# Passes of 512 weight columns in the second block's values and output projections

## The chip, the cores and the metric

The kernel runs on one core of one Trainium2 chip. The metric is the device time of one execution in microseconds (us); the median of several runs is compared.

## The reference

One sequence of 256 tokens of width 1024 goes through two blocks in float32. The first block (adaptive norm, a mixer of three kinds of attention, a convolutional feed-forward part) isn't touched by the change. The second block is two layers, each with a residual and a layer norm:

```python
def second_block(x, gla_w_in, ..., ln_g, ln_b):
    for layer in range(DEPTH_2):                       # DEPTH_2 = 2
        if layer < N_A_LAYERS:                         # N_A_LAYERS = 1
            y = gla_mixer(x, ...)
        else:
            if layer == N_A_LAYERS:
                k_sh, v_sh = shared_kv(x, w_kv)
            y = dilated_mixer(x, swa_w_in[i], swa_w_out[i], k_sh, v_sh)
        x = layer_norm(DEEPNORM_ALPHA * x + y, ln_g[layer], ln_b[layer])

def gla_mixer(x, w_in, w_a2, b_a2, norm_g, w_out):
    proj = x @ w_in                                    # q 512, k 512, v 1024, g 1024, a_lr 16
    log_a = jax.nn.log_sigmoid(a_lr @ w_a2 + b_a2) / 16
    o = gla_chunked(q, k, v, log_a)                    # 4 heads, chunks of 64 tokens, a decaying state
    o = o * lax.rsqrt(jnp.mean(o * o, axis=-1, keepdims=True) + RMS_EPS)
    return (o * norm_g * jax.nn.silu(g)) @ w_out

def shared_kv(x, w_kv):
    k, v = jnp.split(x @ w_kv, [768], axis=-1)         # 3 groups x 2 heads x 128, each
    return rope(k, pos), v

def dilated_mixer(x, w_in, w_out, k_sh, v_sh):
    q, g = jnp.split(x @ w_in, [3072], axis=-1)        # 3 groups x 8 heads x 128, and the gate
    ...                                                # windowed attention with dilation 1, 4, 16
    return (o * jax.nn.silu(g)) @ w_out
```

## The kernel before

All weights are read from HBM in chunks of about 1 MB (128 partitions x 2048 elements), in an order fixed in `STREAM`, into a ring of four buffers `raw`. To compute in fp32r with the accuracy of float32, each chunk is split in two: ScalarE (ACT) copies it rounded to `whi` (`high`, L639), VectorE (DVE) computes the remainder `wlo = raw - whi` (`low`, L1052). The activations are split the same way (`hhi`/`hlo`, `gohi`/`golo`, `ohi`/`olo`). TensorE (PE) then adds three products per tile (`three`, L1596 to L1598): high by high, low by high, high by low. There are three pairs of split buffers (chunk c uses `whi[c % 3]`, but chunk GOUT+3 uses `wgo` and the last chunk `hhi`/`hlo`) and three result banks `res0` to `res2` in PSUM, taken in turn. `bank(r)` (L1600) lets PE wait until result r-3 has been drained by ACT or DVE. `FIRST_RESULT`, `RESULT_MARK`, `RESULT_DRAIN` and `CHUNK_MARK` (L119 to L134) are the counts of the semaphores `product_done`, `drained_act` and `drained_dve` on which everybody waits.

A chunk is 1024 rows by 256 columns. It makes 48 passes on PE: in `fm` the weights are stationary and the 256 tokens move (the result has features on partitions); in `tm` a tile of 128 tokens is stationary and the 256 weight columns move, once for each of two token tiles, so that the result has tokens on partitions. The chunks of the second block, in order: GK (2), GA, GQ (2), GV (4, values), GG (4, gates), GOUT (4, output projection), SK (3, shared keys), SV (3, shared values), SWA (16, queries and gates), SOUT (4, output projection). GV, GOUT, SV and SOUT have tokens as their stationary tile.

Every engine has its own program, a loop over the chunks in the order above; what stands in it ahead of an instruction is always done first. ACT's step for chunk c is the weight copy of chunk c+3, then what drains result c. In the GV stage PE also makes four transposes (L1974) after GV+2 and the small products of the attention within 16-token blocks (L1982) after GV+3, for which DVE has to finish the factors `gfacs`; ACT computes their exponentials (L900, L903) between the copies, and the copy `kdT` (L906). In the GOUT stage PE first adds the residual by products with the identity (`residual`, L1722) to each bank. The token tiles are normalised one after the other (`rows_normed`, `row_sum`, `row_squares`), transposed back by PE (`hidden`, L1730) and split again (L710, L1479) before SK can begin; 23 products that nobody reads (`warm`, L1644) lie between the end of tile 1 and its transposes.

```python
            def bank(r):
                if r >= DIRECT + NB:
                    who, n = RESULT_DRAIN[r - NB]
                    pe.wait_ge(drained[who], n)
                return res[r % NB]
```

## Time and profile before

| what | value |
|---|---|
| median of 3 runs | 753.12 us (752.69 to 759.79) |
| profiled execution, first to last instruction | 757.1 us |
| PE busy | 730.8 us (97%) |
| weight loads busy | 710.5 us (94%) |
| DVE busy | 524.7 us (69%) |
| ACT busy | 396.1 us (52%) |
| GpSimd busy | 104.3 us (14%) |
| read from HBM | 139.17 MB, 185 GB/s over the span |

The profiled execution is one of its own; of it the span is known, and it is 4 us above the median of the runs. Durations below are from it. A matmul's duration in the trace is its latency, and the next one starts before it ends, so what a pass costs is read from the distance of two starts. A plain f32 product appears as two records.

### The profile page before, as it was taken

How to read it: one execution, taken by the hardware profiler on the slowest of the kernel's cores; microseconds unless marked ns; L12 is line 12 of the kernel's file. 1: busy time of each engine (PE TensorE's matmuls, PEld its weight loads, DVE VectorE, ACT ScalarE, POOL GpSimd, SP SyncE). 2: the span in 40 equal slices, each digit the busy share in tenths (PEclk: the TensorE clock that was granted, in tenths of full speed). 3: DMA queues.
4: the chain of work that ended last, by engine and by line, in shares of the span. 5: the costliest groups of instructions: out<-in, count | busy, mean ns of one | idle time of the engine just before them, and what ended most of it. 6: DMA issues, size and time to landing. Idle time of an engine off the chain costs nothing.

```text
span 757.1 us, 14222 instructions
## 1 busy us (share of the span) xinstructions
PE 730.8 (97%) x5964; PEld 710.5 (94%) x5964; DVE 524.7 (69%) x778; ACT 396.1 (52%) x560; POOL 104.3 (14%) x87
## 2 busy tenths in 40 slices
PE   8899999998899999999999999999999999999995
PEld 6799899898898999999999989899999999999995
DVE  4979888886977678777767556925576347555665
ACT  4286455545364544544544348528555456556551
POOL 0130000000522000000001130000004455443000
PEclk9999999999999999999999999979999999999998
DMA  8995567555363455654566544514446553343101
GB/s 343 411 356 190 203 268 274 193 204 219 113 244 146 167 200 190 213 178 161 204 261 233 205 138 148 207 66 168 167 154 223 184 206 117 116 159 112 57 1 56
DMA packets 22265, 141.13 MB, mean 186 GB/s; under 512 B 2389, under 2 KB 3029, under 8 KB 6458
## 3 DMA queue, kind: packets, MB, share of 16 engines
q1 hardware_dynamic: 21626, 137.28, 50.1%
q0 software_dynamic: 576, 2.95, 1.0%
q8 instruction: 47, 0.77, 0.4%
q14 instruction: 16, 0.13, 0.1%
HBM read 139.17 MB, written 1.05 MB: 185 GB/s over the span
## 4 chain that ended last, share of the span: by engine, by line
PE 70%; DVE 13%; issue 7%; ACT 5%; DMA 3%; POOL 0%; SPq 0%; DVEq 0%; ACTq 0%
PE res L1596 20%; PE res L1598 19%; PE res L1597 19%; ACT whi L639 3%; DVE wlo L1052 3%; PE pX L1803 2%; DMA shared<-in_w_ada 1%; PE pS L1783 1%; PE pX L1982 1%; DVE shared L1065 1%; DVE raw L1065 1%; DMA y<-in_w_ada 1%; ACT sq L654 1%; PE pT L1793 1%; PE pS L1644 1%
## 5 line engine op out<-in xcount | busy, mean ns | idle before, releaser
L1596 PE MATMUL res<-hhi,whi 128*128 128x256 f32 (+1 forms) x1120 | 318.9, 285 | 4.1 <-DVE wlo L1052 1.5
L1052 DVE TENSOR_TENSOR wlo<-raw,whi 128x2048 fp32r<-128x2048 f32 (+3 forms) x101 | 229.1, 2270 | 126.4 <-ACT whi L639 126.2
L1597 PE MATMUL res<-hhi,wlo 128*128 128x256 f32 (+1 forms) x1120 | 312.9, 279 | 0.0
L1598 PE MATMUL res<-hlo,whi 128*128 128x256 f32 (+1 forms) x1120 | 312.8, 279 | 0.0
L639 ACT ACTIVATE whi<-raw 128x2048 fp32r<-128x2048 f32 (+3 forms) x101 | 188.3, 1865 | 120.2 <-issue 87.1
L1596 PEld LDWEIGHTS res<-hhi,whi 128*128 128x128 f32 (+1 forms) x1120 | 209.6, 187 | 5.9 <-issue 3.4
L1597 PEld LDWEIGHTS res<-hhi,wlo 128*128 128x128 f32 (+1 forms) x1120 | 209.4, 187 | 0.4
L1598 PEld LDWEIGHTS res<-hlo,whi 128*128 128x128 f32 (+1 forms) x1120 | 209.4, 187 | 0.2
L538 POOL TENSOR_TENSOR sq<-sq,rope 128x512 f32<-128x512 f32 x18 | 39.5, 2195 | 78.5 <-ACT sq L654 78.5
L1596 PE MATMUL res<-uhi,whi 128*128 128x256 f32 x176 | 49.3, 280 | 0.0
L1597 PE MATMUL res<-uhi,wlo 128*128 128x256 f32 x176 | 49.1, 279 | 0.0
L1598 PE MATMUL res<-ulo,whi 128*128 128x256 f32 x176 | 49.1, 279 | 0.0
L1065 DVE CUSTOM_DVE_ANT_0 raw<-raw,cact,cols 128x1024 f32<-128x1024 f32 x32 | 41.8, 1344 | 0.0
L1596 PE MATMUL res<-whi,hhi 128*128 128x256 f32 x144 | 40.5, 281 | 0.0
L1597 PE MATMUL res<-whi,hlo 128*128 128x256 f32 x144 | 40.1, 278 | 0.0
L1598 PE MATMUL res<-wlo,hhi 128*128 128x256 f32 x144 | 40.1, 278 | 0.0
L1598 PEld LDWEIGHTS res<-ulo,whi 128*128 128x128 f32 x176 | 33.1, 188 | 0.0
L1596 PEld LDWEIGHTS res<-uhi,whi 128*128 128x128 f32 x176 | 33.0, 188 | 0.0
L1597 PEld LDWEIGHTS res<-uhi,wlo 128*128 128x128 f32 x176 | 32.9, 187 | 0.0
L560 POOL TENSOR_TENSOR sq<-sq 128x512 f32<-128x512 f32 x4 | 7.6, 1902 | 182.6 <-ACT sq L863 167.0
L802 ACT ACTIVATE up<-shared,unmax 128x128 f32<-128x128 f32 (+1 forms) x24 | 10.9, 456 | 41.4 <-DVE unmax L1207 41.4
L576 POOL TENSOR_TENSOR y<-y,sq 128x512 f32<-128x512 f32 x8 | 10.5, 1351 | 140.4 <-DVE sq L1227 140.4
(334 smaller groups left out, 1211.1 us busy)
## 6 DMA issues: line engine op xcount, KB each, us to landing
raw<-in_wts SPq DMA_DIRECT2D x97, 1024.0 KB, 5.0
raw<-in_w_ada SPq DMA_DIRECT2D x16, 1024.0 KB, 5.1
shared<-in_w_ada SPq DMA_DIRECT2D x6, 1024.0 KB, 11.1
gates<-in_wts SPq DMA_DIRECT2D x4, 768.0 KB, 13.3
raw<-in_wts SPq DMA_DIRECT2D x4, 768.0 KB, 5.6
y<-in_w_ada SPq DMA_DIRECT2D x2, 1024.0 KB, 9.2
x<-in_xT SPq DMA_DIRECT2D x2, 512.0 KB, 4.7
gv<-in_ln_rows POOLq DMA_DIRECT2D x1, 1024.0 KB, 7.5
```

The lines of the kernel that those rows point to most:

```text
L538: nc.gpsimd.tensor_tensor(xsw, xsw, table[:, 1:2, :].to_broadcast([P, 2, T]), ALU.mult).then_inc(sin_done, 1)
L560: nc.gpsimd.tensor_tensor(sq[:, 0:2, :], sq[:, 0:2, :], sq[:, a:a + 2, :], ALU.add).then_inc(presummed, 1)
L576: nc.gpsimd.tensor_tensor(y[:, 2 * j:2 * j + 2, :], y[:, 2 * j:2 * j + 2, :], gtmp[:, n % 4, :].rearrange("p (a b) -> p a b", a=2), ALU.ad ...
L639: nc.scalar.activation(hi[:, 0:kt * w], raw[RAW_OF["w", c] % RAW][:, 0:kt * w], ACT.Copy).then_inc(hi_ready, 1)
L654: nc.scalar.activation(swapped(c)[a:a + block_rows, :, :].rearrange("p a b -> p (a b)"), ps[b:b + block_rows, :], ACT.Copy).then_inc(moved ...
L802: nc.scalar.activation(up[:, s % 3, 0:nk], usc[:, s % 2, 0:nk], ACT.Exp, scale=-1.0, bias=unmax[:, s % 4:s % 4 + 1], accum_out=uden[:, s % ...
L1052: nc.vector.tensor_tensor(lo[:, 0:b], raw[RAW_OF["w", c] % RAW][:, 0:b], hi[:, 0:b].bitcast(f32), ALU.subtract).then_inc(lo_ready, 1)
L1065: nc.vector.tensor_tensor_reduce(out=w[:, D * i:D * i + D], in0=w[:, D * i:D * i + D], in1=cact[:, :], op0=ALU.mult, op1=ALU.add, scale=1. ...
L1596: mm(out, ah, bh, start=first, stop=False)
L1597: mm(out, al, bh, start=False, stop=False)
L1598: return mm(out, ah, bl, start=False, stop=last)
L1803: last = mm(pX[:, T + P * t:T + P * t + P], v, dpT[:, t, P * i:P * i + P], start=i == 0, stop=i == 3)
```

## The change

In GV, GOUT, SOUT and the first two chunks of SV a chunk is now 512 rows (four k-tiles) by 512 columns, in place of 1024 rows by 256. A pass moves 512 columns, so a pair of chunks needs 48 passes where it needed 96, and fills one whole bank for each token tile. A result is complete after the second chunk of a pair: the first chunk of a GV or SV pair marks no result (`results_of` is 0), the second marks two. ACT moves both results of a pair after it. GOUT keeps tile 0's and tile 1's first halves open together for six k-tiles, then finishes tile 0's first half, its second half, tile 1's first half, its second half. SOUT goes k-tile by k-tile over both token tiles for the first 512 columns, then tile by tile. The sums of the layer norm are made over 512 columns at once in place of twice 256. Removed lines are left out of the diff where the old functions above show them.

```diff
@@ -84,7 +84,14 @@
         return 2, 1024
     if DOWN <= c < GK:
         return (8, 8, 6)[(c - DOWN) % 3], 256
+    if in_rows(c):
+        return 4, 512
     return KT, 256
+
+
+def in_rows(c):
+
+    return GV <= c < GG or GOUT <= c < SK or SV <= c < SV + 2 or SOUT <= c
 
 
 def results_of(c):
@@ -93,7 +100,9 @@
         return 4
     if DOWN <= c < GK:
         return 2 if (c - DOWN) % 3 == 2 else 0
-    return 2 if c == SK - 1 else 1
+    if GV <= c < GG or SV <= c < SV + 2:
+        return 2 * ((c - (GV if c < GG else SV)) % 2)
+    return 1
 
 
...
@@ -130,7 +139,7 @@
     CHUNK_MARK.append(_m)
 
 
-CHUNK_MARK[GOUT + 1] = RESULT_MARK[FIRST_RESULT[GOUT + 3]]
+CHUNK_MARK[GOUT] = CHUNK_MARK[GOUT + 1] = CHUNK_MARK[GOUT + 2]
 CHUNK_MARK[GOUT + 2] = CHUNK_MARK[GOUT + 3]
 
...
@@ -196,16 +205,18 @@
         return cols(gla_in, 3072, 16)
     if c < GV:
         return cols(gla_in, 256 * (c - GQ), 256)
+    if in_rows(c):
+        m, first, a = ((gla_in, GV, 1024) if c < GG else (gla_out, GOUT, 0) if c < SK else
+                       (w_kv, SV, 768) if c < SWA else (swa_out, SOUT, 0))
...
@@ -883,11 +894,11 @@
                     own(nc.scalar.activation(gla, glz, ACT.Abs))
                     own(nc.scalar.activation(gla, gla, ACT.Exp, scale=-1.0))
                     nc.scalar.activation(gla, gla, ACT.Ln, bias=1.0).then_inc(loga_ready, 1)
-                if GV <= b < GG:
-                    j = b - GV
-                    ps = result(FIRST_RESULT[b])
-                    nc.scalar.activation(gv[:, :, 256 * j:256 * j + 256], ps[:, :].rearrange("p (t n) -> p t n", t=2),
-                                         ACT.Copy).then_inc(drained_act, 1)
+                if b in (GV + 1, GV + 3):
+                    j = (b - GV) // 2
+                    for t in range(2):
+                        ps = result(FIRST_RESULT[b] + t)
+                        nc.scalar.activation(gv[:, t, 512 * j:512 * j + 512], ps[:, :], ACT.Copy).then_inc(drained_act, 1)
                 if b == GV - 1:
 
...
@@ -943,32 +954,24 @@
                         act.wait_ge(go_full, i + 1)
                         nc.scalar.activation(gohi[:, 2 * i:2 * i + 2, :], y[:, 2 * i:2 * i + 2, :], ACT.Copy).then_inc(go_hi, 1)
                 if b == GOUT:
+                    load_root()
+                if b in (GOUT, GOUT + 2):
+                    t = (b - GOUT) // 2
+                    row_sum(result(FIRST_RESULT[b])[:, :], t, 0, 512, 0).then_inc(drained_act, 1)
+                    act.wait_ge(z_shift, t + 1)
+                    row_squares(z[:, t, 0:512], t, 0, 3).then_inc(z_squared, 1)
+                    if t:
+                        high(SK)
+                        hidden_high(0)
+                if b in (GOUT + 1, GOUT + 3):
+                    t = (b - GOUT) // 2
                     ps = result(FIRST_RESULT[b])
+                    row_sum(ps[:, :], t, 512, 512, 2).then_inc(z_summed, 1)
+                    row_squares(ps[:, :], t, 512, 4).then_inc(drained_act, 1)
+                    row_root(t, 0)
+                    if t:
+                        hidden_high(1)
+                        high(SK + 1)
                 if b == SOUT + 1:
                     load_root()
...
@@ -1481,18 +1485,18 @@
 
                 if b == GOUT:
                     low(c + 2)
+                if b in (GOUT, GOUT + 2):
+                    t = (b - GOUT) // 2
+                    dve.wait_ge(drained_act, RESULT_DRAIN[FIRST_RESULT[b]][1])
+                    shift_of(t)
+                    if t:
+                        low(SK)
+                        hidden_low(0)
                 if b == GOUT + 1:
                     dve.wait_ge(rows5_in, 16)
                     dve.wait_ge(xe_ready, 1)
                     rows_normed(0, 0, gv, x_rows, x_rows_ready)
                 if b == GOUT + 3:
                     rows_normed(1, 0, gv, x_rows, x_rows_ready)
                     hidden_low(1)
...
@@ -1505,14 +1509,12 @@
                     low(c + 2)
                     dve.wait_ge(x_ready, 2)
                 if SOUT <= b < SOUT + 2:
+                    t = b - SOUT
+                    row_add(result(FIRST_RESULT[b])[:, :], t, 0, 512, 0).then_inc(drained_dve, 1)
                     dve.wait_ge(drained_dve, RESULT_DRAIN[FIRST_RESULT[b]][1])
+                    shift_of(t)
+                    if t:
+                        dve.wait_ge(rows_in, 16)
                 if b >= SOUT + 2:
                     t = b - SOUT - 2
...
@@ -1711,10 +1713,22 @@
                     last = mm(out, meanw[:, :], sq[:, k, :], start=False, stop=k == 7)
                 last.then_inc(mean_known[n], 1)
 
-            def token_product(ps, at, t, k, ih, il, wh, wl, first, last):
-
-                return three(ps[:, at:at + T], ih[:, k, t * P:t * P + P], il[:, k, t * P:t * P + P],
-                             wh[:, k, :], wl[:, k, :], first, last)
+            def rows_product(ps, t, first_c, k, ih, il, first, last):
+
+                wh, wl = weights_of(first_c + k // 4)
+                return three(ps[:, :], ih[:, k, t * P:t * P + P], il[:, k, t * P:t * P + P],
+                             wh[:, k % 4, :], wl[:, k % 4, :], first, last)
+
+            def rows_chunk(c, first_c):
+
+                wait_weights(c)
+                r, kg = FIRST_RESULT[first_c + 1], c - first_c
+                for t in range(2):
+                    ps = res[(r + t) % NB] if kg else bank(r + t)
+                    for k in range(4 * kg, 4 * kg + 4):
+                        last = rows_product(ps, t, first_c, k, hhi, hlo, k == 0, k == KT - 1)
+                    if t or kg:
+                        last.then_inc(product_done, 1)
 
             def residual(ps, at, t, ks):
...
@@ -2004,43 +2018,38 @@
                     r = FIRST_RESULT[GOUT]
                     if c == GOUT:
                         pe.wait_ge(xe_ready, 1)
+                        first = bank(r), bank(r + 2)
                         for t in range(2):
+                            residual(first[t], 0, t, range(4))
+                            for k in range(6):
+                                if k % 4 == 0:
+                                    wait_weights(GOUT + k // 4)
+                                pe.wait_ge(go_lo, k // 2 + 1)
+                                rows_product(first[t], t, GOUT, k, gohi, golo, False, False)
+                        pe.wait_ge(go_lo, 4)
+                    if c in (GOUT, GOUT + 2):
+                        t = (c - GOUT) // 2
+                        for k in (6, 7):
+                            last = rows_product(first[t], t, GOUT, k, gohi, golo, False, k == 7)
+                        last.then_inc(product_done, 1)
+                    if c in (GOUT + 1, GOUT + 3):
+                        t = (c - GOUT) // 2
+                        ps = bank(FIRST_RESULT[c])
+                        residual(ps, 0, t, range(4, KT))
                         for k in range(KT):
+                            if k % 4 == 0:
+                                wait_weights(GOUT + 2 + k // 4)
+                            last = rows_product(ps, t, GOUT + 2, k, gohi, golo, False, k == 7)
+                            if t and k == 5:
+                                hidden(0)
                         last.then_inc(product_done, 1)
+                        if t:
+                            warm(23, ident, pX[:, 0:P])
+                            hidden(1)
                 elif c < SOUT:
+                    if SV <= c < SV + 2:
+                        rows_chunk(c, SV)
+                    elif c == SV + 2:
                         tm(c, hhi, hlo)
                     else:
...
@@ -2050,22 +2059,22 @@
                 else:
                     r = FIRST_RESULT[SOUT]
                     if c == SOUT:
+                        first = [bank(r + t) for t in range(2)]
                         for k in range(KT):
+                            if k % 4 == 0:
+                                wait_weights(SOUT + k // 4)
                             pe.wait_ge(d_lo, k // 2 + 1)
+                            for t in range(2):
+                                last = rows_product(first[t], t, SOUT, k, ohi, olo, k == 0, k == 7)
+                                if k == 7:
                                     last.then_inc(product_done, 1)
                     if c == SOUT + 2:
                         for t in range(2):
                             ps = bank(r + 2 + t)
+                            for k in range(KT):
+                                if k % 4 == 0:
+                                    wait_weights(SOUT + 2 + k // 4)
+                                last = rows_product(ps, t, SOUT + 2, k, ohi, olo, k == 0, k == 7)
                             last.then_inc(product_done, 1)
```

ACT's row in the GV stage, before; `whi2<-raw0` is the weight copy for GV+3, `whi0<-raw1` that for GG, `gfacs` with 3072 elements the exponential, `gv<-res1` the move of GV's result:

```order
L639 ACTIVATE whi2<-raw0 128x2048 [waits lo_ready,product_done,raw_full0]
L889 ACTIVATE gv<-res1 128x2x256 [waits product_done]
L903 ACTIVATE gfacs<-gfacs 128x3072 [waits gdiff]
L639 ACTIVATE whi0<-raw1 128x2048 [waits lo_ready,product_done,raw_full1]
L889 ACTIVATE gv<-res2 128x2x256 [waits product_done]
L639 ACTIVATE whi1<-raw2 128x2048 [waits lo_ready,product_done,raw_full2]
L889 ACTIVATE gv<-res0 128x2x256 [waits product_done]
L906 ACTIVATE kdT<-pT 128x512 [waits kd_T]
```

And now:

```order
L650 ACTIVATE whi2<-raw0 128x2048 [waits lo_ready,product_done,raw_full0]
L914 ACTIVATE gfacs<-gfacs 128x3072 [waits gdiff]
L650 ACTIVATE whi0<-raw1 128x2048 [waits lo_ready,product_done,raw_full1]
L901 ACTIVATE gv<-res1 128x512 [waits product_done]
L901 ACTIVATE gv<-res2 128x512 [waits product_done]
L650 ACTIVATE whi1<-raw2 128x2048 [waits lo_ready,product_done,raw_full2]
L917 ACTIVATE kdT<-pT 128x512 [waits kd_T]
```

The move of GV's result no longer stands ahead of the exponential; both results of the first pair are moved behind it and behind the weight copy for GG.

PE from chunk GV+2 on, now; `res0` and `res1` are the banks of its two token tiles, L1988 are the four transposes, and `...` stands for passes of the same kind:

```order
L1598 MATMUL res0<-whi1,hhi 128x512 [waits drained_act,lo_ready]
L1599 MATMUL res0<-whi1,hlo 128x512
L1600 MATMUL res0<-wlo1,hhi 128x512
...
L1600 MATMUL res0<-wlo1,hhi 128x512
L1598 MATMUL res1<-whi1,hhi 128x512 [waits drained_act]
L1599 MATMUL res1<-whi1,hlo 128x512
L1600 MATMUL res1<-wlo1,hhi 128x512
...
L1988 MATMUL pT<-ident,gfacs 128x128 [waits gfac]
L1988 MATMUL pT<-ident,gfacs 128x128 x3
L1598 MATMUL res0<-whi2,hhi 128x512 [waits lo_ready]
```

The second token tile waits for `drained_act`, that is, for the move out of `res1` just shown; before, GV+2 took one bank for both tiles and waited once.

PE at the start of GOUT, before; the first row is the last pass of GG+3:

```order
L1598 MATMUL res2<-hlo,whi0 128x256
L1722 MATMUL res0<-ident,xe 128x128 [waits drained_act,xe_ready]
L1722 MATMUL res0<-ident,xe 128x128 x3
L1596 MATMUL res0<-whi1,gohi 128x256 [waits go_lo,lo_ready]
L1597 MATMUL res0<-whi1,golo 128x256
L1598 MATMUL res0<-wlo1,gohi 128x256
```

And now:

```order
L1600 MATMUL res2<-hlo,whi0 128x256
L1736 MATMUL res0<-ident,xe 128x128 [waits drained_act,xe_ready]
L1736 MATMUL res0<-ident,xe 128x128 x3
L1598 MATMUL res0<-whi1,gohi 128x512 [waits go_lo,lo_ready]
L1599 MATMUL res0<-whi1,golo 128x512
L1600 MATMUL res0<-wlo1,gohi 128x512
```

The wait for `drained_act` at the first residual is now for two banks, that of tile 0 (`res0`) and that of tile 1 (`res2`, which holds the result of GG+3); before it was for `res0` alone.

## Rows read from the trace of the kernel before

**Rows 1.** The page: busy time of each engine, and the granted clock in 40 slices.
```profile
PE 730.8 (97%) x5964; PEld 710.5 (94%) x5964; DVE 524.7 (69%) x778; ACT 396.1 (52%) x560; POOL 104.3 (14%) x87
...
PEclk9999999999999999999999999979999999999998
```

**Rows 2.** Busy times of stretches: busy us (x instructions) of PE, PEld, DVE, ACT, POOL, PEclk, DMA, GB/s.
```profile
240.00:340.00 100.00, 100.00 (x851) 100.00 (x850) 76.79 (x92) 51.96 (x50) 3.80 (x5) 1.00 0.52 180
...
464.00:486.00 22.00, 20.94 (x183) 20.74 (x182) 21.97 (x22) 17.11 (x15) 0.00 (x0) 1.00 0.54 175
...
590.00:625.00 35.00, 35.00 (x297) 34.91 (x296) 16.27 (x12) 17.51 (x18) 15.13 (x9) 1.00 0.54 187
```

**Rows 3.** Plain f32 products of 256 columns: timeline row, and durations min/median/max in ns.
```profile
514.78 1.89 PE L1811 MATMUL pT<-tb,headw 128*128 128x256 f32 x8
...
L1811 PE MATMUL pT<-tb,headw x8: 378/379/379, 514.8 to 516.3; 128*128 128x256 f32 x8
```

**Rows 4.** Timeline of ACT (start us, us, engine, line, operation, idle before and releaser), 472 to 481.
```profile
472.92 0.57 ACT L889 ACTIVATE gv<-res 128x512 f32<-128x512 f32 x1
...
475.46 2.78 ACT L903 ACTIVATE gfacs<-gfacs 128x3072 f32<-128x3072 f32 x1 [1.97 <-DVE gfacs L1376]
...
478.14 1.91 ACT L639 ACTIVATE whi<-raw 128x2048 fp32r<-128x2048 f32 x1
...
479.95 0.58 ACT L889 ACTIVATE gv<-res 128x512 f32<-128x512 f32 x1
```

**Rows 5.** Timeline of PE at the end of GV+2 and the start of L1982.
```profile
478.00 0.28 PE L1596 MATMUL res<-whi,hhi 128*128 128x256 f32 x1
...
478.34 0.28 PE L1596 MATMUL res<-whi,hhi 128*128 128x256 f32 x1
...
478.69 0.60 PE L1974 MATMUL pT<-ident,gfacs 128*128 128x128 f32 x4
...
486.37 10.32 PE L1982 MATMUL pX<-qI,gfacs 128*16 128x16 f32 x125 [1.43 <-DVE gfacs L1400]
```

**Rows 6.** Busy times of stretches around the two falls of the granted clock.
```profile
498.30:500.10 1.80, 1.80 (x10) 1.76 (x9) 1.77 (x10) 0.00 (x0) 0.00 (x0) 0.51 0.00 0
...
749.60:752.60 3.00, 0.00 (x0) 0.00 (x0) 2.70 (x9) 1.11 (x3) 0.00 (x0) 1.00 0.34 127
...
752.80:757.00 4.20, 0.00 (x0) 0.00 (x0) 1.73 (x4) 0.00 (x0) 0.00 (x0) 0.50 0.34 125
```

**Rows 7.** PE's waits: waited for, us in total, times, longest us.
```profile
PE res L1596 <- ACT gates L779: 1.9, 1, 1.9
```

**Rows 8.** Timelines of PE and ACT at the start of the gated layer's output projection.
```profile
530.64 1.05 PE L1722 MATMUL res<-ident,xe 128*128 128x128 f32 x8
...
532.53 0.63 ACT L944 ACTIVATE gohi<-y 128x512 fp32r<-128x512 f32 x1 [2.48 <-DVE y L1438]
...
533.55 0.83 ACT L921 ACTIVATE gs<-res,ggh 128x256 f32<-128x256 f32 x2
```

**Rows 9.** Timelines of PE, ACT and DVE at the end of both token tiles.
```profile
546.91 0.61 PE L1722 MATMUL res<-ident,xe 128*128 128x128 f32 x4
...
557.76 0.60 ACT L696 ACTIVATE tb<-res 128x512 f32<-128x512 f32 x1 [1.42 <-PE res L1598]
...
557.61 1.28 DVE L1479 TENSOR_TENSOR hlo<-pS,hhi 128x512 fp32r<-128x512 f32 x2
...
558.81 0.20 DVE L1452 TENSOR_SCALAR zs<-zs 128x1 f32<-128x1 f32 x1
```

**Rows 10.** Timelines of PE and DVE in the last projection.
```profile
726.17 0.28 PE L1596 MATMUL res<-whi,ohi 128*128 128x256 f32 x1
...
749.02 0.28 PE L1598 MATMUL res<-hlo,ohi 128*128 128x256 f32 x1
...
743.72 0.69 DVE L1501 CUSTOM_DVE_ANT_0 tb<-res,x 128x512 f32<-128x512 f32 x1 [3.98 <-PE res L1598]
...
749.34 0.69 DVE L1501 CUSTOM_DVE_ANT_0 tb<-res,x 128x512 f32<-128x512 f32 x1 [0.33 <-PE res L1598]
```

More of the change, by code:

```diff
@@ L1457, in rows_normed @@
                     if base == 0:
-                        dve.wait_ge(drained_act, RESULT_DRAIN[FIRST_RESULT[SK - 1] + t * 2 - 1][1])
+                        dve.wait_ge(drained_act, RESULT_DRAIN[FIRST_RESULT[GOUT + 1 + 2 * t]][1])
                     else:
@@ L2006, in _ @@
                         pe.wait_ge(xe_ready, 1)
-                        ps = bank(r)
+                        first = bank(r), bank(r + 2)
                         for t in range(2):
-                            residual(ps, T * t, t, (0, 1))
-                        wh, wl = weights(c)
-                        for k in range(KT):
-                            pe.wait_ge(go_lo, k // 2 + 1)
-                            for t in range(2):
-                                last = token_product(ps, T * t, t, k, gohi, golo, wh, wl, False, k == KT - 1 and t == 1)
-                            if k == 5:
-                                ps1 = bank(r + 1)
-                                residual(ps1, 0, 0, (2, 3))
-                                nh, nl = weights(GOUT + 1)
-                                for kk in range(6):
-                                    token_product(ps1, 0, 0, kk, gohi, golo, nh, nl, False, False)
@@ L2052, in _ @@
                     if c == SOUT:
-                        first = [bank(r + d) for d in range(2)]
-                        both = [weights(SOUT + d) for d in range(2)]
+                        first = [bank(r + t) for t in range(2)]
                         for k in range(KT):
+                            if k % 4 == 0:
+                                wait_weights(SOUT + k // 4)
                             pe.wait_ge(d_lo, k // 2 + 1)
-                            for d in range(2):
-                                for t in range(2):
-                                    last = token_product(first[d], T * t, t, k, ohi, olo, *both[d], k == 0 and t == 0, k == KT - 1 and t == 1)
-                                if k == KT - 1:
+                            for t in range(2):
+                                last = rows_product(first[t], t, SOUT, k, ohi, olo, k == 0, k == 7)
+                                if k == 7:
                                     last.then_inc(product_done, 1)
@@ L2064, in _ @@
                             ps = bank(r + 2 + t)
-                            for d in range(2):
-                                wh, wl = weights(SOUT + 2 + d)
-                                for k in range(KT):
-                                    last = token_product(ps, T * d, t, k, ohi, olo, wh, wl, d == 0 and k == 0, d == 1 and k == KT - 1)
+                            for k in range(KT):
+                                if k % 4 == 0:
+                                    wait_weights(SOUT + 2 + k // 4)
+                                last = rows_product(ps, t, SOUT + 2, k, ohi, olo, k == 0, k == 7)
                             last.then_inc(product_done, 1)
```

79 lines of the change are left out of this document (9 added, 70 removed).

## The prediction

> **What bounds the kernel now.** The profiled execution spans 757.1 us; the median of the runs is 753.1 us. I work out differences in the profiled execution and put them on the median. I read five views, in this order. First the page's busy line: TensorE (PE) is busy 97% of the span, its granted clock is full in nearly every slice, and VectorE (DVE) and ScalarE (ACT) reach 69% and 52% [rows 1]. So whatever PE does faster counts, where PE is what a stage waits for. The busy times of single stretches say where that is: from 240 to 340 and from 590 to 625 PE never rests, but in 464 to 486 it is DVE that is busy 21.97 of 22.00 us, and PE already has gaps [rows 2]. Then the timeline of ACT and DVE around the places where results leave PSUM, since the change alters how long a result bank is held. Then PE's waits, and last the granted clock in and after its pauses.
>
> **The pass of 512 columns.** The change replaces two 256-column passes over the same stationary tile by one of 512 columns. It removes 96 passes from the values of the gated layer (chunks GV), 96 from its output projection (GOUT), 48 from the shared values (SV) and 96 from the last projection (SOUT): 336. A 256-column pass costs 117.5 ns from start to start: 851 of them in 100 us [rows 2]. In SOUT it is (749.02 - 726.17) / 191 = 119.6 ns [rows 10]. No row shows a 512-column pass in this number format. The nearest are the plain f32 products of 256 columns, which the trace records twice each: eight records take 1.89 us, of which the last is 0.38 long [rows 3], so one costs (1.89 - 0.38) / 7 = 215.7 ns. The bound from above is two short passes, 235 ns. The bound from below is 512 columns at the full clock of 2.4 GHz, 213 ns, for at one column a cycle even the short passes are above their 107. I take 215.7, the measured row. Each pair then gives 19.3 ns, and 23.5 in SOUT: 240 x 19.3 + 96 x 23.5 = 6.9 us if all of it counted.
>
> The Trainium skill ("TensorE: Matmul & The Clock Gate", section "Back-to-back issue gap") puts a warm pass at its columns by 2.4 GHz plus about 2.5 ns: 109.2 ns for 256 columns and 215.8 for 512. The f32 rows agree with the second number; the short passes, at 117.5, don't agree with the first. By that rule a pair would give 2.6 ns and all 336 together 0.9 us. The short passes of this kernel are measured, so the sum goes by their rows.
>
> **GV: two banks are held, and PE waits.** Before, each chunk of 256 columns fills one of three result banks, and ACT moves it out right away. Now two chunks, each with half the rows of 512 columns, fill two banks, one per token tile, and both are moved only after the second chunk. The second token tile of the next pair (chunk GV+2) takes the bank of the first pair's first tile. Its move stands in ACT's queue behind the exponential at L903 and the weight copy for chunk GG. The exponential waits for a factor from DVE; it runs from 475.46 to 478.24, the copy to 480.05, the move to 480.53 [rows 4]. Nothing of this depends on PE's pace, since DVE is busy throughout. PE ends GV+2 at 478.69 now; three passes take 0.34 us here, so three chunks of 48 take 16.3 and GV begins at 462.4 [rows 5]. With long passes PE does two chunks (48 x 215.7 ns = 10.35 us) and half of GV+2 (2.59) until 475.3, and then stands until 480.6: a pause of 5.3 us that isn't there today. From 480.6 it needs 2.59 for the other half, 0.35 for four transposes and 5.18 for GV+3, so it reaches L1982 at 488.7. Today L1982 starts at 486.37, after 1.43 us of waiting for DVE [rows 5]. That is 2.35 us later. The faster passes of this stage would by themselves only have made that wait longer.
>
> **The clock after the pause.** Today PE's longest wait under way is 1.9 us [rows 7], and the clock is full through it. After PE's last product it is still full in 749.6 to 752.6 and at the lower level, 1.2 GHz, from 752.8 on [rows 6]. A pause of 5.3 us is longer than that stretch, so I expect a fall in it. In 498.3 to 500.1, the first 1.8 us of dense work after the small products of L1982, the granted clock is still 0.51 [rows 6]; as much of dense work at half rate is a loss of 0.9 us. The bounds are nothing, if no fall comes, and 2.5 us, if half rate lasts 5 us. I take 0.9. The Trainium skill (the same page, section "HAM oscillation — how this bites in real kernels") says that waits between bursts of products can throttle the clock again and again; the end of this trace agrees, and nothing in the sum hangs on it.
>
> **GOUT: a bank asked for too early.** The new code asks for the banks of both token tiles before its first residual product. The second is the bank of the last gate chunk (GG+3). ACT empties that late: its queue holds a copy that waits for DVE's product at L1438 until 532.53, then tanh, then two scaled copies from 533.55 to 534.38. PE could start the residual at 530.64 [rows 8]. It waits 3.7 us. Before, that bank was first asked for by tile 0's second half, many passes later. Another fall of the clock is possible here; the pause is about as long as the stretch after the last product in which the clock held. I leave it out of the sum and price it among the rivals.
>
> **GOUT: the order within.** After tile 0's second half come steps of ACT and DVE in a fixed row: sums and normalisation of tile 0, shift and squares of tile 1, ACT's weight copy for SK, DVE's remainder of it and of tile 0's rows, and only at 558.81 the normalisation of tile 1. ACT's sum of tile 1 ends at 558.36 [rows 9], so DVE is already what that waits for. The start of SK thus follows tile 0's end, not tile 1's. From the first residual, tile 0 now takes 120 short passes and 20 residual records, 546.91 - 530.64 = 16.3 us [rows 8, 9]. It will take 66 long passes (14.24) and 24 residual records of (1.05 - 0.28) / 7 = 0.11 us [rows 8] (2.64), 16.9 us, since six k-tiles of tile 1 go ahead. That is 0.6 later. Tile 1's end comes 2.4 us sooner after tile 0's and gains nothing; it leaves PE idle some 2 us more before the transposes of tile 1.
>
> **SV and SOUT: plain gains.** PE is the bound around SV [rows 2], and the banks that SV takes were emptied by DVE long before. 48 pairs by 19.3 ns give 0.9 us, and nothing behind SV catches them. In SOUT 191 starts in 22.85 us become 96 passes in 20.71; with the last pass counted, 22.97 against 20.71, 2.25 less. DVE's work on tile 0 begins at 743.72 and its sum of tile 1 at 749.34, after 0.33 us of waiting for PE [rows 10]: 5.3 us of work. Tile 0 is ready 1.85 us sooner, so DVE is free at 747.2 and PE done at 746.9: of the 2.25 some 2.15 count. Weight chunks stay 1 MB, with the same copies in the same order, and none is needed sooner than before, so transfers and splits cost nothing; if one came late, it would cost its own lateness. The result copies of 128x512 are as long as those of 128x2x256.
>
> **The sum.** GV +2.35, clock +0.9, bank of GOUT +3.7, order of GOUT +0.6, SV -0.9, SOUT -2.15: +4.5, or 757.6. With half a chance of a second fall (0.9) I say **758 us**, 0.6% more.
>
> **Rivals.**
> 1. The clock falls more often and longer: half rate for 5 us after the first pause (+1.6 beyond the sum), a fall at GOUT's pause (+1.3) and one before tile 1's transposes (+1.3), where few products lie between two waits. 753.1 + 4.5 + 4.2 = 762. For it: the clock fell among the small products of L1982 although PE was counted busy. Against: it held over 1.9 us. The point is how long half rate lasts: from 3 us more of it in all the change is 1% slower.
> 2. A long pass costs two short ones, 235 ns. SV and SOUT give nothing, L1982 starts at 489.4 (+3.05), GOUT's tile 0 ends 1.3 us later still: 3.05 + 0.9 + 3.7 + 1.9 = 9.55, 762.7. Against it: rows 3.
> 3. The two waits for banks don't occur, because ACT gets to the moves before PE asks. Then GV gives nothing (DVE), GOUT +0.6, SV -0.9, SOUT -2.15: 750.6, faster than before. Against it: the order of ACT's queue, and that both steps ahead of the moves wait for DVE.
> 4. One of the two waits is half as long, since ACT is relieved of a copy: 755 to 756.
>
> **How the numbers follow.** Forecast 0.50, rivals 0.22, 0.08, 0.10 and 0.10. A measurement of this kernel can tell about 1% (7.5 us) from no change. Over 1% slower is above 760.7: most of the first rival, the second, and a little of the forecast's edge, 0.28. Over 1% faster has no case of its own, 0.02. Within 1%: 0.70. The range of 754 to 763 holds the forecast with its bounds and the first, second and fourth rival; it leaves out the third and the tails.
>
> **What would show it.** In the profile after: 336 passes fewer; long passes 216 ns from start to start; PE waits some 5 us for ACT's move of the gated values within GV+2, and no longer for DVE before L1982; PE waits 3 to 4 us for ACT's scaled copy before the first residual; the clock is low in or after the first of these; SOUT lasts 20.7 us. Without the two waits I am wrong about the banks and the third rival holds; with 235 ns a pass, the second.

## The result, and the profile after

The changed kernel takes 771.2 us (median of four runs, 764.7 to 772.0), the kernel before 756.5 beside it (752.7 to 760.0): ratio 1.0198, 95% interval 1.0145 to 1.0252. Both kernels' times fall in two groups about 6 us apart; in the profiles that is the pace of the short passes between 250 and 445 us, far from the change (see long_turned). Before had two of its four runs in the lower group, the changed kernel one, which makes 14.7 us between the medians; group by group it is 11.8 and 11.7. Both profiled executions ran that stretch at the slow pace, so their spans compare: 757.1 and 768.9 us, 11.8 apart. Below I divide the kernel at PE's starts, from the first pass of GQ to the last pass of SOUT, and so leave that stretch out.

The page, after [rows 1]: 336 passes fewer, 3.2 us more of PE busy, and a lower clock in two slices in the middle where before had one.

```profile
span 768.9 us, 13543 instructions
...
PE 734.0 (95%) x5628; PEld 696.7 (91%) x5628; DVE 524.3 (68%) x774; ACT 395.9 (51%) x556; POOL 104.4 (14%) x87
...
PEclk9999999999999999999999999789999999999998
```

PE's waits, after [rows 7]. All three are new.

```profile
PE res L1598 <- ACT gv L901: 4.4, 1, 4.4
PE res L1736 <- ACT gs L932: 3.7, 1, 3.7
...
PE pT L1744 <- DVE x L1476: 1.6, 1, 1.6
```

ACT's and PE's timelines in GV, after [rows 4, 5]; the small products are at L1996 now.

```profile
475.80 2.77 ACT L914 ACTIVATE gfacs<-gfacs 128x3072 f32<-128x3072 f32 x1 [2.45 <-DVE gfacs L1380]
478.47 1.89 ACT L650 ACTIVATE whi<-raw 128x2048 fp32r<-128x2048 f32 x1
480.27 1.06 ACT L901 ACTIVATE gv<-res 128x512 f32<-128x512 f32 x2
```

```profile
475.90 0.40 PE L1599 MATMUL res<-whi,hlo 128*128 128x512 f32 x1
476.13 0.39 PE L1600 MATMUL res<-wlo,hhi 128*128 128x512 f32 x1
480.90 0.79 PE L1598 MATMUL res<-whi,hhi 128*128 128x512 f32 x1 [4.38 <-ACT gv L901]
481.49 0.63 PE L1599 MATMUL res<-whi,hlo 128*128 128x512 f32 x1
481.92 0.63 PE L1600 MATMUL res<-wlo,hhi 128*128 128x512 f32 x1
...
491.46 10.47 PE L1996 MATMUL pX<-qI,gfacs 128*16 128x16 f32 x125
```

ACT had waited 2.45 us for DVE, with the two results ready for most of it, then ran the exponential and the weight copy ahead of their moves, as [rows 4] let one foresee. Behind the pause the starts are 0.43 us apart, where 475.90 and 476.13 show 0.23: half clock. The windows show it at three places, with a full one at the end for comparison [rows 2, 6]:

```profile
481.10:484.40 3.30, 3.30 (x9) 2.58 (x10) 3.30 (x4) 0.23 (x1) 0.00 (x0) 0.52 0.60 176
...
539.20:542.50 3.30, 2.99 (x12) 2.78 (x13) 2.08 (x3) 1.82 (x3) 0.00 (x0) 0.53 0.33 139
576.70:580.00 3.30, 3.23 (x15) 3.26 (x16) 2.19 (x2) 3.30 (x2) 0.00 (x0) 0.52 0.36 149
752.00:760.00 8.00, 8.00 (x36) 6.45 (x35) 3.89 (x13) 1.40 (x5) 0.00 (x0) 1.00 0.00 0
```

In the kernel before none of these falls is there; the one among the small products [rows 6] is in both. PE in GOUT and SOUT, after [rows 8 to 10]:

```profile
539.51 2.05 PE L1736 MATMUL res<-ident,xe 128*128 128x128 f32 x8 [3.71 <-ACT gs L932]
...
567.66 5.30 PE L1646 MATMUL pX<-ident 128*128 128x128 f32 x46
574.61 1.32 PE L1744 MATMUL pT<-ident,x 128*128 128x128 f32 x8 [1.65 <-DVE x L1476]
576.77 0.55 PE L1598 MATMUL res<-hhi,whi 128*128 128x256 f32 x1 [0.84 <-DVE hlo L1483]
...
738.55 0.40 PE L1598 MATMUL res<-whi,ohi 128*128 128x512 f32 x1
...
760.75 0.40 PE L1600 MATMUL res<-hlo,ohi 128*128 128x512 f32 x1
```

SOUT's 96 passes have 95 steps in 22.20 us: **233.7 ns** each, not 215.7. The 191 steps of before took 22.85.

The stages of all versions, from starts in their traces (us): GQ's first pass to the first small product, to the first residual product, to SK's first pass, to SOUT's first, to SOUT's last; and the sum. Behind it the runs' median. The versions were timed in several sessions, in which the median of before moved between 753.1 and 759.1 us with the mix of the two groups, so the medians of different sessions don't compare; the sums of the stages do.

```
              GQ-small -residual    -SK    -SOUT   -last     sum   median
before           37.55    44.27   34.19   161.34   22.85  300.20
after            42.20    48.05   37.26   161.78   22.20  311.49   771.2
split            42.18    48.15   37.41   162.78   22.85  313.37   769.7
early_moves      37.55    49.30   37.46   161.90   22.20  308.41   764.8
late_bank        43.19    44.41   35.88   163.05   22.20  308.73   764.1
both             37.55    45.41   35.88   160.41   22.19  301.44   755.8
warm_fit         40.78    48.27   35.95   160.39   22.19  307.58   760.9
high_first       37.54    44.46   34.01   160.50   22.19  298.70   758.3
sv_sout          37.45    45.31   34.08   160.49   22.20  299.53   757.2
gv_old           37.55    44.37   34.00   160.43   22.19  298.54   753.5
same_twice       37.56    44.36   35.88   162.93   22.20  302.93   755.1
long_turned      37.54    45.50   34.09   160.09   22.85  300.07   762.1
best             37.55    44.36   34.00   160.40   22.19  298.50   761.3
four_turned      37.44    45.58   34.00   160.49   22.19  299.70   754.6
```

### The profile page after: what moved, and what is told of

The parts are those of the page before. It is cut to its first block and busy times, and to the rows that moved or that the text cites. A ratio compares the mean times of both kernels' runs of the same rounds, so it can differ in the third digit from the quotient of the medians.

```text
span 768.9 us, 13543 instructions
## 1 busy us (share of the span) xinstructions
PE 734.0 (95%) x5628; PEld 696.7 (91%) x5628; DVE 524.3 (68%) x774; ACT 395.9 (51%) x556; POOL 104.4 (14%) x87
## 5 line engine op out<-in xcount | busy, mean ns | idle before, releaser
L1598 PE MATMUL res<-whi,hhi 128*128 128x256 f32 (+1 forms) x96 | 33.5, 349 | 4.4 <-ACT gv L901 4.4
L1599 PE MATMUL res<-whi,hlo 128*128 128x256 f32 (+1 forms) x96 | 32.8, 342 | 0.0
L1600 PE MATMUL res<-wlo,hhi 128*128 128x256 f32 (+1 forms) x96 | 32.7, 340 | 0.0
```

Of the source, the lines that this page charges most:

```text
L1598: mm(out, ah, bh, start=first, stop=False)
L1599: mm(out, al, bh, start=False, stop=False)
L1600: return mm(out, ah, bl, start=False, stop=last)
```

## Experiments

**split.** Is the long pass itself what is slow?

```diff
-  three(ps, token tile, 512 weight columns)
+  for each of the three: mm(ps[:, 0:256], ...); mm(ps[:, 256:512], ...)
```

> The changed kernel with each pass of 512 weight columns cut into two of 256 one after the other; chunks, banks, order and waits stay. Theory (a long pass costs as much as two short ones, about 233 ns in the trace of the changed kernel, and the loss lies in two bank waits and the clock): the same time as the changed kernel, within 2 us of its 771 us, pauses of 4.4 and 3.7 us at the same places. Rival 1 (the long pass is itself what is slow, because 512 columns run worse than two times 256): 4 to 8 us faster than the changed kernel, since 336 long passes go from 233 ns to 2 x 113 or less. Rival 2 (a long pass is cheaper than two short ones even if less than forecast): 2 to 6 us slower than the changed kernel.

Measured: 769.7 us, ratio to before 1.0196 (1.0124 to 1.0268), as the changed kernel's. Same pauses (4.4 and 3.7), the same three falls, SOUT back at 22.85 us. A long pass thus buys 0.65 us in all of SOUT, and the 11 us by which the change is slower than before are not of the pass: they come with the order in which banks are held and asked for. (What the pass costs against the forecast is another question; see the next section.) The stages add up to 1.9 us more than the changed kernel's, near the edge of the 2 us that I allowed: 0.65 in SOUT and 1.0 behind SK, where the short passes ran at the slower pace.

**early_moves, late_bank, both.** Take away each wait.

```diff
 early_moves (ACT)
-  b == GV:      high(c + 2); exponential L914
-  b == GV + 1:  high(c + 2); move two results
+  b == GV:      high(c + 2)
+  b == GV + 1:  move two results; high(c + 2); exponential
 late_bank (PE)
-  first = bank(r), bank(r + 2)
+  for t in range(2): first.append(bank(r + 2 * t)); ...
```

> The changed kernel with ACT moving the two results of the first values pair ahead of the 2.8 us exponential and of the high part of the chunk two on, in the time in which it now waits for VectorE. Theory (bank wait plus clock): the pause of 4.4 us in the third values chunk goes, the fall of the granted clock that followed it (3.4 us at half) goes with it, 1.4 us of an old wait for VectorE ahead of the 128 small products may come back: 4.5 to 6 us less, about 766. Rival 1 (the clock falls there for another reason): only 3 to 4 us less. Rival 2 (ACT's exponential is then late and VectorE's products on it take over): less than 2 us gained, with a new wait for VectorE of 3 us or more ahead of the small products.

> The changed kernel with the second bank of the gated projection asked for only behind the 18 long passes of token tile 0. Theory: the 3.7 us wait goes, since the bank comes free at 539.4 us of the span and token tile 1 is reached at about 540.4; the fall of the clock behind it goes too: 5 to 5.5 us less, about 766. Rival 1 (the clock falls there anyway): 3.5 us less. Rival 2 (the gated rows or the weight halves are the next wait): less than 2 us less, and a wait on golo or wlo of 2 to 4 us in the place of the one on gs.

> The changed kernel with both moves. Theory: their gains add, 10 to 11 us less than the changed kernel, about 760 to 761, so about 1 us above the kernel before at the same level: the rest is the idle time ahead of token tile 1's transposes with its fall of the clock, and no gain from the passes. Rival 1 (passes of 512 columns are dearer here than two of 256 elsewhere too): still 4 us or more above the kernel before. Rival 2 (the passes do gain once nothing waits): 2 us or more below the kernel before.

Measured: 764.8, 764.1 and 755.8 us; ratios 1.0136 (1.0042 to 1.0230), 1.0107 (1.0025 to 1.0189) and 0.9997 (0.9957 to 1.0037). In both, the small products wait for DVE again and GQ to there is 37.55 us, exactly as before the change, so GV's long passes are worth nothing:

```profile
487.12 1.04 PE L1997 MATMUL pX<-qI,gfacs 128*16 128x16 f32 x15 [1.02 <-DVE gfacs L1405]
```

early_moves wins 4.65 us in GV and loses 1.25 among the small products, where the clock's fall was longer (13.7 us, 10.2 in before and after). late_bank wins 3.6 to the residual and 1.4 to SK; its other stages have longer falls than after's (6.8 us twice), which is why its sum is only 2.8 lower. So the stages give 3.1 us for early_moves, where I expected 4.5 to 6, and 2.8 for late_bank, where I expected 5 to 5.5: each wait went and its own fall with it, but other falls were longer in these executions. In both, 10.0 us of the 11.3 are gone, and 1.2 us above before are left, as expected.

**warm_pauses, warm_fit.** Keep both waits, but fill them.

```diff
+  if c == GV + 2 and t == 1: warm(19, ident, pX[:, 0:P])     # warm_pauses: 36
   ps = ... bank(r + t)
...
+  warm(16, ident, pX[:, 0:P])                                # warm_pauses: 30
   first = bank(r), bank(r + 2)
```

> The changed kernel with both bank waits kept, but filled: 36 products of 128 columns on the identity (0.11 us each, into a bank that nobody reads) ahead of the first, 30 ahead of the second. No wait gets shorter. Theory (a pause costs its length and then a fall of the granted clock, 3.4 us at half): the falls at 481.1 and 539.1 us go, the products behind them begin at the same time and run at full clock: 3 to 3.4 us less than the changed kernel, about 768. Rival 1 (the falls come at fixed times whatever PE does): no change. Rival 2 (the fill is longer than the waits): 0 to 2 us more.

> The changed kernel with both bank waits filled to their own length: a product on the identity is recorded twice and takes 0.22 us, so 19 and 16 of them, 4.3 and 3.6 us. Theory (a pause costs its length and then a fall of the granted clock): from the first chunk of the stage at 449 us to the start of SK 124 us, where the changed kernel took 127.5, since the two falls at 481.1 and 539.1 us go; 3.4 us less in all. Rival (the falls were not of the pauses): 127 us or more.

warm_pauses measured 768.5 us (ratio 1.0156, 1.0082 to 1.0230) and says little of time: a product on the identity is two records of 0.11 us, so the fills were twice as long as the waits. The falls were gone, though. With fills of the right length, warm_fit measured 760.9 (1.0116, 1.0045 to 1.0187), and its granted clock is full over both places:

```profile
476.00:484.00 8.00, 8.00 (x36) 6.51 (x37) 7.95 (x8) 2.84 (x3) 0.00 (x0) 1.00 0.54 194
536.00:543.00 7.00, 7.00 (x36) 5.81 (x35) 4.50 (x3) 4.37 (x4) 0.00 (x0) 1.00 0.37 117
```

PE begins no pass earlier for a filled wait, yet GQ to the small products falls by 1.4 us and residual to SK by 1.3: that is what the two falls cost. It isn't the chance of one profile: the mean granted clock is 0.977 to 0.984 in all eight runs of after and split, and 0.985 to 0.991 in all eight of the two filled versions. GQ to SK is 125.0 us against 127.5; I expected 124. The third fall, behind tile 1's transposes, isn't there either (160.39 against 161.78), although the 1.65 us pause ahead of them stayed.

**high_first.** What makes PE wait ahead of tile 1's transposes?

```diff
   row_sum(tile 1, first half)
+  if t: high(SK)
   act.wait_ge(z_shift, t + 1)
   row_squares(...)
-  if t: high(SK)
```

> The version with both bank waits removed, and in the gated projection ACT makes the weight copy for SK ahead of its wait for VectorE's shift of token tile 1, where it stood 2.1 us idle, in place of behind the squares. Theory (the 1.65 us in which PE waits ahead of token tile 1's transposes come from ACT and VectorE reaching tile 1's normalisation late): 1.2 to 1.7 us less, SK begins 33.0 us or less behind the first residual, where it was 35.9. Rival 1 (VectorE, not ACT, sets it): under 0.5 us. Rival 2 (the copy delays ACT's sums of tile 1): up to 1 us slower.

Measured: 758.3 us, ratio 0.9993 (0.9955 to 1.0031); residual to SK 34.01 us against 35.88, 1.9 less where I expected 1.2 to 1.7 (the 33.0 that I also wrote doesn't follow from that and didn't come), and no wait ahead of the transposes. ACT's copy now fills its own wait, and DVE begins tile 1's normalisation behind ACT's sum instead of behind its own queue:

```profile
553.73 1.91 ACT L650 ACTIVATE whi<-raw 128x2048 fp32r<-128x2048 f32 x1
555.91 0.73 ACT L711 ACTIVATE sq<-tb,zs 128x512 f32<-128x512 f32 x1 [0.27 <-DVE zs L1450]
```

```profile
559.86 0.21 DVE L1458 TENSOR_SCALAR zs<-zs 128x1 f32<-128x1 f32 x1 [0.56 <-ACT tb L707]
```

**sv_sout, gv_old.** Change only stages without a bank wait; and all but GV, with the two repairs of GOUT.

```diff
 sv_sout
-  in_rows(c): GV <= c < GG or GOUT <= c < SK or SV <= c < SV + 2 or SOUT <= c
+  in_rows(c): SV <= c < SV + 2 or SOUT <= c
 gv_old
+  in_rows(c): GOUT <= c < SK or SV <= c < SV + 2 or SOUT <= c
```

> The kernel before with only SV and SOUT changed, where no bank wait stands in the way. By the forecast's price of a long pass (216 ns) 3.0 us less than the kernel before; by the price in the trace after (232 to 233 against 119 ns a short pass) SOUT takes 22.2 us in place of 22.85 and SV gains 0.2 to 0.5: 1 us less, which a comparison of times can't tell from none. Rival (the long pass is dearer than two short ones away from pauses): slower, SOUT 23 us or more.

> The values of the gated layer as before the change (256 columns, one bank a chunk), the other three stages changed, with the later bank and ACT's copy for SK ahead of its wait. Theory (GV has nothing to gain, since VectorE sets the start of the 128 small products): from the pause-free start of the stage at about 442 or 449 us to the first small product 37.5 us as in the kernel before; the whole 1 to 3 us below the kernel before at the same pace of the short passes. Rival 1 (long passes in GV are worth something once nothing waits): 1 us or more slower than the version with all four stages and the same other edits. Rival 2 (their early end feeds the fall of the clock among the small products): 1 to 2 us faster than that version.

Measured: 757.2 us, 0.9978 (0.9939 to 1.0017), and 753.5 us, 0.9962 (0.9918 to 1.0006), against 759.1 for before beside them. The stages give 0.7 and 1.7 us. By the stages gv_old is only 0.2 us shorter than high_first (298.5 and 298.7), so GV with long or short passes is the same; their medians, 4.9 us apart, differ by how many of the ten runs fell in which group. gv_old is the shortest of the versions without added products, but its interval touches 1. SOUT takes 22.2 us as I then expected, and SK to SOUT gains 0.85 in sv_sout, more than the 0.2 to 0.5 that I expected; most of it isn't the long passes' own (see the next section).

**same_twice, probe.** What is the price of a long pass made of?

```diff
 same_twice (on both)
-  high x high, low x high, high x low
+  high x high, high x low, low x high     (stationary x weights)
 probe (on gv_old, behind the last product of SOUT)
+  32 passes of 512 columns; 32 of 256; 32 of 512 on one stationary tile
+  8 plain f32 products of 512 columns
```

> The version with both bank waits removed, and in each k-tile the two long passes that use the same stationary tile one after the other (high by high, high by low, low by high). Theory (232 ns is the price of the pass of 512 columns in this format, however the stationary tile alternates): SOUT stays at 22.2 us, no difference in time. Rival (the change of the stationary tile is what adds 17 ns to the 216 of the forecast): a third of the passes is 10 to 17 ns shorter, SOUT 21.7 us or less.

> The version with GV as before, the three other stages changed, the later bank and ACT's copy for SK ahead of its wait, and behind its last product 104 more on TensorE whose result nobody reads, while the other engines finish: 32 passes of 512 columns in the format of the weights, 32 of 256, 32 of 512 that all use one stationary tile, and 8 plain f32 products of 512 columns. Their starts give the price of a pass by itself. Theory 1 (the price belongs to the format: so much a column): about 232 ns a long pass and 116 to 118 a short one here too, and f32 at 2 x 216 or more. Theory 2 (the weight stream, buffers in use by other engines or the residuals make it 232): 216 to 220 ns for the long passes, at least with one stationary tile. Theory 3 (a pass costs its columns and a fixed part): the short one at 113 or less, the long one at 220 or less.

Measured: same_twice 755.1 us, 1.0041 (1.0002 to 1.0080), SOUT 22.20 us, as in both: which product follows which makes no difference, as the theory said. probe ran once, 775.8 us with its added work; its timeline:

```profile
747.92 7.63 PE L2084 MATMUL pS<-whi,ohi 128*128 128x512 f32 x32
755.39 4.00 PE L2086 MATMUL pS<-whi,ohi 128*128 128x256 f32 x32
759.23 7.63 PE L2088 MATMUL pS<-whi,ohi 128*128 128x512 f32 x32
```

and the durations of each group, in which the f32 products are recorded twice each, as in [rows 3]:

```profile
L2084 PE MATMUL pS<-whi,ohi x32: 392/394/399, 747.9 to 755.2; 128*128 128x512 f32 x32
...
L2086 PE MATMUL pS<-whi,ohi x32: 278/282/286, 755.4 to 759.1; 128*128 128x256 f32 x32
...
L2090 PE MATMUL pS<-dsc,ident x16: 592/592/592, 766.7 to 773.1; 128*128 128x512 f32 x16
```

(7.63 - 0.39) / 31 = 233.5 ns a long pass, with or without a changing stationary tile; (4.00 - 0.28) / 31 = 120 a short one; the 16 f32 records span 7.03 us, so (7.03 - 0.59) / 15 = 429 an f32 record. The trace has a weight load ahead of every pass in both groups of 512, so a stream without loads is not shown. The weight stream, the buffers and the residuals weren't needed for 233: of the three theories the first holds.

**long_turned, best, four_turned.** What puts executions into two groups of times? Between 250 and 445 us some profiles have one pace and some the other, at full clock in both. 45 us of gv_old, and below them the same 45 us of long_turned:

```profile
255.00:300.00 45.00, 45.00 (x400) 45.00 (x399) 36.73 (x44) 24.87 (x23) 0.00 (x0) 1.00 0.54 192
```

```profile
255.00:300.00 45.00, 45.00 (x384) 45.00 (x384) 36.70 (x45) 23.12 (x22) 0.00 (x0) 1.00 0.57 191
```

```diff
 turned(c), three products ahead of the third chunk of UP and of WOUT
-  3 of 256 columns
+  6 of 512 columns      (long_turned on before, best on gv_old)
+  12 of 256 columns     (four_turned on gv_old)
```

> The kernel before, and nothing of the change: only the three extra products of 256 columns that stand in the fourth chunk of the square projection and in the third of the gated hidden layer (their result is not read) become six of 512 columns, at both places. In every profile so far that has long passes in SV, the short passes behind them run at 113 ns until other products come between, in place of 118; in the stretch of 1700 short passes from 250 to 445 us some executions run at 113 and others at 118, 6.2 us apart, and times fall in two groups. Theory (long passes bring TensorE's stream of short ones into the faster pace, and the two groups of times are this stretch): the stretch is at 113 ns in the profile, and all runs fall in the lower group, about 751 to 755 us, where the kernel before has half of its runs at 758 to 762: median 4 to 6 us less. Rival 1 (it was chance, or only long work does it): both groups stay, no difference in the mean. Rival 2 (the groups come from something else): 113 ns in the profile, but two groups still. Cost of the edit: 1.4 us.

> The version with GV as before, the three other stages changed, the later bank, ACT's copy for SK ahead of its wait, and the six products of 512 columns at the two places. Theory: 1.6 us below the kernel before at the same pace, always at the faster pace, less 1 us for the added products: 749 to 752 in all runs, ratio 0.985 to 0.993 to the kernel before. Rival (the pace doesn't follow): 750 to 760 in two groups as the same version without the added products.

> The same version with twelve products of 256 columns in place of three at the two places where six of 512 kept every run in the upper group of times. Theory (at this place the three products may or may not bring the stream of short passes from 118 to 113 ns, and more of them try more often): all runs in the lower group, 749 to 754. Rival 1 (any added work there keeps the pace at 118): all runs in the upper group, 758 to 762. Rival 2 (no influence): two groups as before.

Measured: long_turned 762.1 us (1.0119, 1.0081 to 1.0158), best 761.3 (1.0096, 1.0057 to 1.0134), four_turned 754.6 (0.9997, 0.9958 to 1.0037). My theory that long passes bring the faster pace was wrong, the opposite came: all twelve runs of the first two lie in the upper group (759.0 to 764.9), with the slow pace in both profiles. four_turned's lie at 753.7 to 755.3 ten times and at 761.7 to 761.8 twice. That this stretch makes the two groups is well supported: every profile agrees (113 ns where its own run lies in the lower group of its version, 118 in the upper), and an edit at its head moved whole sets of runs. Why these products set the pace isn't known, and best is not the version to keep.

## Why the prediction was wrong

I forecast 758 us, within 754 to 763; it was 771. By its steps:

- **The pass of 512 columns: 215.7 ns taken, 233 measured. This step failed.** My own bound from above, 235, was right. A record of an f32 product of 256 columns is not a stand-in for 512 columns of the weights' format: probe shows the f32 record at 429 ns for 512 columns, nearly twice the other's 233. The price follows the format's columns: 233 against two short passes at 235 to 240, and at the faster pace of the short ones, 113 to 115 in the GV stage of before, two of them at 226 to 230 are cheaper than the long one. The rule of the Trainium skill that I weighed ("TensorE: Matmul & The Clock Gate", section "Back-to-back issue gap") gives 215.8 ns for 512 columns as the gap of an isolated product, and says that it over-counts at large sizes in a stream with weight loads; here it under-counts, 215.8 against 233, and 109.2 against 113 to 120 for 256 columns. That my f32 rows agreed with its 215.8 was chance: they are of 256 columns, and the number is for 512. At 17.3 ns a pass, SOUT gave 0.65 us instead of 2.15, GV's 36 long passes behind the pause cost 0.6 more and the 66 ahead of tile 0's end in GOUT 1.1 more.
- **GV's bank wait: right.** Forecast 5.3 us, measured 4.4, because the 60 long passes ahead of it, 17.3 ns dearer each, bring PE there 1.0 us later; its end, 480.9, lies 0.3 us from where I put it. The waiting order in ACT's queue was as described, and early_moves removed it.
- **The clock: the direction right, the number and size wrong.** I summed 0.9 us and half a chance of a second fall. There were three, at half rate for 3.4 us each: 1.4, 1.3 and 1.4 us (warm_fit and the SK column). The first two follow the pauses of 4.4 and 3.7 us, and filling these removed them, so that cause is shown. The third follows the pause of 1.65 us, but not in every version that has it, so its cause is open. The first rival had all three places; I gave it 0.22.
- **GOUT's bank: right**, 3.7 us forecast and measured; late_bank took it away.
- **GOUT's order: mechanism right.** With the clock's fall set aside, residual to SK grew by 1.69 us (both against before). 0.6 forecast and 1.1 for the dearer passes is 1.7. PE idled 1.65 us ahead of tile 1's transposes, as said. I took this chain as given; high_first shows that one step in ACT's order removes it.
- **SV: right by accident.** Forecast -0.9, measured -0.93 in both. By their price its 48 long passes give about 0.1. Nearly all comes from the short passes behind SV, which ran at the faster pace for 26 us (232 starts where before had 222). That pace came in every profile whose SV has long passes, and neither in before nor in split, whose SV has short ones; but it also came in long_turned, whose SV is unchanged. So long passes in SV may bring it and aren't needed for it; the cause isn't shown.
- **The sum of rivals.** Rivals 1 and 2 both came true. They were priced as if one excluded the other: 9.55 us and another 4.2 on 753.1 make 766.9, outside the range. That was the second mistake, of the chances.
- **The anchor.** I put the differences, read from a profiled execution of the upper group (757.1 us), on a median of 753.1 that lay in the lower group. The changed kernel's median lay in the upper one. The measured difference of 11.8 put on 753.1 gives 764.9, and the median was 771.2: of the 13.2 us by which I missed, 6.3 are this and 6.9 the difference itself. Even without it, 764.9 would lie outside my 754 to 763.

In all: 11.8 measured against 4.9 forecast. Of the 6.9 between them, 3.3 are the price of the pass, 2.75 the clock (4.1 against 1.35); 0.4 lie ahead of GQ, and 0.4 are small pieces. That 26 us stretch behind SV, in both and then in the kernel before:

```profile
597.00:623.00 26.00, 26.00 (x232) 26.00 (x231) 12.76 (x8) 14.51 (x14) 9.27 (x6) 1.00 0.56 198
```

```profile
597.00:623.00 26.00, 26.00 (x222) 25.96 (x222) 11.63 (x8) 13.02 (x12) 10.39 (x6) 1.00 0.54 179
```

## What to carry to other kernels

Wider passes save little when the format's price grows with its columns; measure one pass in the format itself before costing a change by another format's row. What a wider pass changes is how long result banks are held: read the draining engine's queue at every point where a bank is asked for, and ask for it last. A wait of PE costs its length and, where the clock falls behind it, over a microsecond more; here unneeded products in the wait gave that back, but moving the drain ahead of an unrelated step, or asking for the bank later, gave back all.

## What the runs showed of the hardware

- A long pass in the weights' format takes 233 ns even behind the end of the kernel's own work and with an unchanged stationary tile, a short one 120 there, an f32 record of 512 columns 429 (probe).
- The same pause of 1.6 to 1.7 us ahead of tile 1's transposes was followed by a fall of the clock in after, split, early_moves, late_bank and same_twice, and by none in both, warm_fit and warm_pauses.
- Among the small products the half clock lasted 10.2 us in some executions and 13.7 in others; the stage to the residual is then 44.3 to 44.5 or 45.3 to 45.6 us.
- A stream of short passes has two paces at full clock, 113 and 118 ns, and keeps one until other work comes between; a few products at its head move the choice, which is worth 6 us to this kernel. What decides is open.
